# One branch on the count instead of four, over a loop through the four general passes

## What is computed

```python
h = h + moe(rmsnorm(h, g_ffn[l]), w_router[l], router_bias[l], w_gate[l], w_up[l],
            w_down[l], ws_gate[l], ws_up[l], ws_down[l])
return rmsnorm(h, g_final)
```

## Time and profile before

| | us |
|---|---|
| runs (3) | 1243.57, 1249.34, 1250.41 |
| median | 1249.34 |
| profiled execution, its own time | 1247.41 |
| its span, first to last instruction | 1245.6 |
| TensorE busy | 1100.4 (88%) |
| VectorE busy | 400.5 (32%) |
| ScalarE busy | 221.3 (18%) |
| GpSimd busy | 147.3 (12%) |
| mean granted clock of TensorE | 0.951 of full speed |

### The profile page before, as it was taken

How to read it: one execution, slowest core, us unless ns; L and a number is a source line. 1 busy time by engine, 2 the same in 40 slices (tenths; PEclk the granted TensorE clock), 3 DMA queues, 4 the chain that set the end, 5 groups by cost and what they waited for, 6 DMA issues and landing times.

```text
span 1245.6 us, 13250 instructions
## 1 busy us (share of the span) xinstructions
PE 1100.4 (88%) x5027; PEld 528.2 (42%) x5027; DVE 400.5 (32%) x927; ACT 221.3 (18%) x481; POOL 147.3 (12%) x194
## 2 busy tenths in 40 slices
PE   5999797887899969997999999997999889989745
PEld 3444585654444454443444343332433333423312
DVE  1883566353212031049522222221112122112127
ACT  3311432344102031031011111111111111101101
POOL 3000006020000000000212122121212111211100
PEclk9999798998899998999999999998999899989979
DMA  6234322320135400333399999999999999999387
GB/s 199 68 102 101 65 102 43 123 81 2 66 133 204 169 34 1 100 135 110 149 408 391 410 419 422 420 421 402 420 419 404 413 410 372 422 396 372 121 323 305
DMA packets 75821, 300.69 MB, mean 241 GB/s; under 512 B 20726, under 2 KB 24091, under 8 KB 50139
## 3 DMA queue, kind: packets, MB, share of 16 engines
q1 hardware_dynamic: 63066, 265.01, 54.7%
q0 software_dynamic: 12672, 34.62, 7.1%
HBM read 282.03 MB, written 27.53 MB: 249 GB/s over the span
## 4 chain that ended last, share of the span: by engine, by line
PE 76%; DMA 9%; DVE 6%; issue 4%; ACT 3%; SPq 1%; POOLq 0%; POOL 0%; DVEq 0%
PE ps L688 25%; PE ps L1070 22%; PE ps L1086 12%; PE ps L1052 3%; DMA ring<-in_w_down 3%; DMA dw<-in_w_down 3%; PE ps L812 2%; DMA ring<-expert_rows 2%; PE ps L825 2%; PE ps L671 1%; PE ps L1032 1%; PE ps L964 1%; PE ps L940 1%; PE ps L1094 1%; DMA z<-in_g_final 1%
## 5 line engine op out<-in xcount | busy, mean ns | idle before, releaser
L1070 PE MATMUL ps<-ring,z 128*32 128x512 f32 (+2 forms) x1056 | 270.9, 597 | 2.5 <-issue 1.3
L688 PE MATMUL ps<-dw,act_t 128*128 128x512 f32 x576 | 249.8, 595 | 3.1 <-issue 2.2
L688 PEld LDWEIGHTS ps<-dw,act_t 128*128 128x128 f32 x576 | 109.5, 191 | 140.0 <-issue 138.9
L1086 PE MATMUL ps<-ring,act_t 128*64 128x512 f32 (+2 forms) x528 | 146.8, 645 | 17.3 <-issue 14.5
L1070 PEld LDWEIGHTS ps<-ring,z 128*32 128x32 f32 (+2 forms) x1056 | 88.2, 134 | 115.4 <-issue 113.2
L1070 PE MATMUL ps<-z 128*32 128x512 f32 (+1 forms) x272 | 80.1, 603 | 4.9 <-issue 4.9
L1070 PE MATMUL ps<-dw,z 128*32 128x512 f32 (+2 forms) x272 | 77.7, 594 | 0.0
L1933 DVE COPY z<-ps 128x512 f32<-128x512 f32 x44 | 30.4, 692 | 139.7 <-PE ps L1086 139.7
L1086 PEld LDWEIGHTS ps<-ring,act_t 128*64 128x64 f32 (+2 forms) x528 | 44.3, 141 | 72.0 <-issue 68.3
L1411 ACT ACTIVATE tok<-ps 128x256 f32<-128x256 f32 x44 | 16.9, 384 | 307.4 <-PE ps L1070 307.4
L2065 POOL COPY ixb<-tabs 128x1 uint32<-128x1 uint32 x88 | 16.7, 190 | 411.1 <-DVE z L1933 393.3
(11 more groups left out here) (304 smaller groups left out, 1225.4 us busy)
## 6 DMA issues: line engine op xcount, KB each, us to landing
ring<-in_w_gate SPq DMA_DIRECT2D x44, 1024.0 KB
ring<-in_w_up SPq DMA_DIRECT2D x44, 1024.0 KB
ring<-in_w_down SPq DMA_DIRECT2D x44, 1024.0 KB, 29.1
ring<-expert_rows SPq DMA_DIRECT2D x8, 2048.0 KB, 21.7
dw<-in_w_gate SPq DMA_DIRECT2D x10, 1024.0 KB, 16.2
dw<-in_w_up SPq DMA_DIRECT2D x10, 1024.0 KB, 29.4
z<-in_w_gate SPq DMA_DIRECT2D x10, 1024.0 KB, 15.0
z<-in_w_up SPq DMA_DIRECT2D x10, 1024.0 KB, 28.5
```

The costliest lines, as they stand in the source:

```text
L688: ins = pe.matmul(ps[0:m, bank0 + j, 0:n], lhs(w, q * 4 + c4, c4, j), rhs(w, q * 4 + c4, c4, j), start=(q == 0 and c4 == 0), stop=(q == le ...
L1070: ins = pe.matmul(ps[rows, 2 + r % 2, :], xtt[r % 2][:, c, rows], ring_wgu(x % NBUF)[:, :, c, :], start=(c == 0), stop=(c == NC_D - 1))
L1086: ins = pe.matmul(ps[rows, 5 + n, :], htt[r % 2][:, c, rows], ring_wd(x % NBUF)[:, c, n * 512:(n + 1) * 512], start=(c == 0), stop=(c == 1))
```

## The change

The four branches of each engine, on the count over 0, 128, 256 and 384, become one branch on the count over 0. Under it stands a loop on the engine (`Fori`) through the four passes, so a pass number is a register's value, and what was worked out from it as a constant becomes sums of registers. If the count is above zero, all four passes run. Where a wait's target is now in a register, semaphore increments have been put behind some waits. On VectorE the table and address steps of a pass move into `pass_table`, which chains its steps by targets that depend on the pass; the calls outside the passes keep their steps, with `link` handed in. The core of the diff:

```diff
-    def slots_needed(eng):
-
-        return eng.value_load(ti[0:1, 0:1], min_val=0, max_val=S)
-
-    def needs_pass(eng, needed, p):
-
-        return eng.If(needed > SLOTS * p)
+    def needs_passes(eng):
+
+        return eng.If(eng.value_load(ti[0:1, 0:1], min_val=0, max_val=S) > 0)
...
         sp.wait_ge(s_cnti, 1)
-        needed = slots_needed(sp)
-        for p in range(PASSES):
-            with needs_pass(sp, needed, p):
-                if p == 0:
-                    sp.wait_ge(e_y, NR)
-                    sp.wait_ge(e_gu, NR)
-                    sp.dma_start(tv[0:NE, :], tvd).then_inc(s_tg, 16)
+        with needs_passes(sp):
+            sp.wait_ge(e_y, NR)
+            sp.wait_ge(e_gu, NR)
+            sp.dma_start(tv[0:NE, :], tvd).then_inc(s_tg, 16)
+            with sp.Fori(0, PASSES) as p:
                 with sp.Fori(0, NE // 4) as it:
                     for j in range(4):
-                        sp.wait_ge(e_y, it * 4 + (NR + NE * p - 3 + j))
+                        sp.wait_ge(e_y, p * NE + it * 4 + (NR - 3 + j))
                         load_expert(sp, it * 4 + j, j)
...
-        needed = slots_needed(pe)
-        for p in range(PASSES):
-            with needs_pass(pe, needed, p):
+        with needs_passes(pe):
+            with pe.Fori(0, PASSES) as p:
                 pe.wait_ge(s_srt, p + 2)
+                pe.sem_inc(s_pc, 1)
                 pe.transpose(ps[:, 0, 0:NE], ts_[0:NE, :], ident[0:NE, 0:NE]).then_inc(s_srf, 1)
                 pe.wait_ge(s_tab, p + 2)
                 one_pass(p)
...
-        needed = slots_needed(act)
-        for p in range(PASSES):
-            with needs_pass(act, needed, p):
+        with needs_passes(act):
+            with act.Fori(0, PASSES) as p:
                 one_pass(p)
...
-        def addresses(p):
-
-            dve.wait_ge(s_srf, p + 1)
-            if p == 0:
-                dve.tensor_copy(ecol, ps[:, 0, NE:NE + NR])
-                dve.tensor_copy(eid[:], ps[0:1, 0, 2 * NE:3 * NE])
-            else:
-                dve.wait_ge(s_idx, 2 * (NR + NE * (p - 1)))
-            n = NE if p else NR
+        def addresses(link, n):
+
...
             if n == 1:
-                addresses(0)
+                dve.wait_ge(s_srf, 1)
+                dve.tensor_copy(ecol, ps[:, 0, NE:NE + NR])
+                dve.tensor_copy(eid[:], ps[0:1, 0, 2 * NE:3 * NE])
+                addresses(link, NR)
...
+        LINKS = 2 * (2 * (SLOTS // 8) - 1 + 2)
+
+        def pass_table(p):
+
+            before, n = steps[0], [0]
+
+            def link_in_pass(ins):
+
+                n[0] += 2
+                ins.then_inc(s_dve, 1)
+                dve.wait_ge(s_dve, p * LINKS + (before + n[0] - 1))
+                dve.sem_inc(s_dve, 1)
+
+            slot_table(link_in_pass)
+            dve.wait_ge(s_srf, p + 2)
+            dve.wait_ge(s_idx, p * (2 * NE) + 2 * NR)
+            addresses(link_in_pass, NE)
+            assert n[0] == LINKS
...
-        needed = slots_needed(dve)
-        for p in range(PASSES):
-            with needs_pass(dve, needed, p):
-                if p == 0:
-                    dve.wait_ge(s_tg, 16 * (NT + 3))
-                slot_table()
-                addresses(p + 1)
+        with needs_passes(dve):
+            dve.wait_ge(s_tg, 16 * (NT + 3))
+            with dve.Fori(0, PASSES) as p:
+                pass_table(p)
                 one_pass(p)
...
         def one_pass(p):
-            base = NR + NE * p
+            base = p * NE + NR
             pool.wait_ge(e_xtr, base)
             pool.wait_ge(e_gc, base)
+            pool.sem_inc(s_gst, 1)
             for b in range(4):
-                gather(b, b, 2 * base + 1 + b)
+                gather(b, b, base * 2 + (1 + b))
...
         pool.wait_ge(s_cnti, 1)
-        needed = slots_needed(pool)
-        for p in range(PASSES):
-            with needs_pass(pool, needed, p):
-                if p == 0:
-                    all_scattered(NR)
+        with needs_passes(pool):
+            all_scattered(NR)
+            with pool.Fori(0, PASSES) as p:
                 pool.wait_ge(s_tab, p + 2)
+                pool.sem_inc(s_gst, 1)
                 one_pass(p)
         pool.sem_inc(s_rows, 1)
```

More of the change, by code:

```diff
@@ L1120, in one_pass @@
         def one_pass(p):
-            base, itb = NR + NE * p, NE // 4 * p
-            pe.wait_ge(xg_ld[0], 16 * (NR // 4 + NE // 4 * p + 1))
+            base, itb = p * NE + NR, p * (NE // 4)
+            pe.wait_ge(xg_ld[0], p * (4 * NE) + 16 * (NR // 4 + 1))
             for c in range(NC_D):
@@ L1129, in one_pass @@
                 for j in range(4):
-                    expert(it * 4 + (base + j), j, it + itb, again[j])
+                    expert(it * 4 + base + j, j, it + itb, again[j])
             for j in range(4):
-                expert(base + NE - 4 + j, j, itb + NE // 4 - 1, again[j], last=(j == 3))
-            down(3, [(ring_dn[3], 16 * (itb + NE // 4 + again[3])), (e_hte, base + NE), (e_yea, base + NE - 1),
-                     (e_yev, base + NE - 1)])
+                expert(base + (NE - 4 + j), j, itb + (NE // 4 - 1), again[j], last=(j == 3))
+            down(3, [(ring_dn[3], itb * 16 + 16 * (NE // 4 + again[3])), (e_hte, base + NE), (e_yea, base + (NE - 1)),
+                     (e_yev, base + (NE - 1))])
         pe.wait_ge(s_tab, 1)
@@ L1430, in one_pass @@
                 for j in range(4):
-                    expert(it * 4 + (base + j), j)
+                    expert(it * 4 + base + j, j)
             for j in range(4):
-                expert(base + NE - 4 + j, j, last=(j == 3))
-            down_out(base + NE - 1, 3)
+                expert(base + (NE - 4 + j), j, last=(j == 3))
+            down_out(base + (NE - 1), 3)
         act.wait_ge(s_tg, 16 * (NT + 2))
@@ L1891, in shared_hidden, with slot_table @@
                                      in1=sha[:, i, :], op0=ALU.mult, op1=ALU.mult).then_inc(s_shh, 1)
-        def slot_table(between=None):
+        def slot_table(link, between=None):
             for q in range(SLOTS // 8):
@@ L1916, in addresses @@
             dve.tensor_scalar(tabs[:, 0, 0:n], tabs[:, 1, 0:n], 3, None, ALU.logical_shift_right).then_inc(s_tab, 1)
-        slot_table(between=(4, 6, 8, 10))
+        slot_table(link, between=(4, 6, 8, 10))
         for n in range(2 * NT):
@@ L1983, in one_pass @@
                 for j in range(4):
-                    expert(it * 4 + (base + j), j, it * 4 + (D + j))
+                    expert(it * 4 + base + j, j, it * 4 + (D + j))
             for j in range(4):
-                expert(base + NE - 4 + j, j, D + NE - 4 + j, last=(j == 3))
-            down_out(base + NE - 1, 3)
+                expert(base + (NE - 4 + j), j, D + NE - 4 + j, last=(j == 3))
+            down_out(base + (NE - 1), 3)
         round_slots(0)
@@ L2114, in all_scattered @@
             for b in range(2):
-                pool.wait_ge(y_out[b], 8 * n)
+                pool.wait_ge(y_out[b], n * 8)
         def one_pass(p):
-            base = NR + NE * p
+            base = p * NE + NR
             pool.wait_ge(e_xtr, base)
             pool.wait_ge(e_gc, base)
+            pool.sem_inc(s_gst, 1)
             for b in range(4):
-                gather(b, b, 2 * base + 1 + b)
+                gather(b, b, base * 2 + (1 + b))
             for j in range(4):
@@ L2126, in one_pass @@
                 for j in range(4):
-                    expert(it * 4 + (base + j), j, it * 4 + j)
+                    expert(it * 4 + base + j, j, it * 4 + j)
             for j in range(4):
-                expert(base + NE - 4 + j, j, NE - 4 + j, tail=True)
+                expert(base + (NE - 4 + j), j, NE - 4 + j, tail=True)
             all_scattered(base + NE)
```

## The result

The changed kernel takes 1239.37 us (median of four runs, 1236.55 to 1240.23). The ratio to the kernel before is 0.9928 with a 95% interval of 0.9905 to 0.9952, so 9.0 us less, between 6.0 and 11.9. A second measurement, among the experiments, gave 0.9912 (0.9878 to 0.9945). The profiled execution spans 1237.3 us, its own time is 1239.09.

What follows compares the result with a forecast made beforehand. GpSimd's four branches were taken to hold the closing loads for 8.24 us, with the scatter's landing next. From 1248.4 us, a 4.85 us gain and nothing elsewhere gave 1243.5 us, 0.39% less; range 1238.5 to 1248.5.

Steps and rivals of the forecast that it cites:

- the sum's own bounds: Gain at the release: 3.2 us with the branch at 5.0 us, 5.05 with 0.42 and a 3.8 us landing.
- What bounds the kernel: Between last round and closing sum: an 11 us hole, where GpSimd's four branches hold the closing phase for 8.24 us.
- Step (a): GpSimd's branches before the closing loads: three of four go; the one left costs 2.58 us (0.42 to 5.0).
- step (b): SP's wait before the closing loads: the last scatter's 4.0 us landing becomes last in, so the gain is 4.85 us.
- Step (c): Branches of VectorE, ScalarE, TensorE and SP: covered or done early, so the same edit there is worth nothing.
- Step (e): First load of rows to the end: no step's work changes, so 56.7 us moves as a whole.
- The fourth rival: Start of the closing loads: less code being fetched there gives at most 1 us on top, 1242.4 us; chance 0.04.
- signs named for "right": Behind the last scatter: one branch per engine, landing ends SP's wait, load 4.1 us behind, 56.7 to end, TensorE 9 behind load.
- Step (d): New code inside the guard: not executed with a count not above zero, so it costs nothing.
- The first, an indirect DMA: GpSimd's queue behind the scatter: slow issue is the DMA's own work, only 0.8 us gained, 1247.6 us; chance 0.08.
- The second, a branch over 3.3 us: GpSimd's remaining branch replaces the landing as last; at 5.0 us the gain is 3.2, time 1245.2 us; chance 0.12.
- the third: GpSimd's remaining branch passes 8.24 us by loading code twice, 10.0 us: 1.8 us later, 1250.2 us; chance 0.03.

Runs made afterwards that it cites:

- all_far: Changed kernel with the four passes written out under the one branch instead of a loop, on every engine; ratio to the kernel before 0.9958 (0.9932 to 0.9984).
- pool_one: Kernel before with GpSimd's part alone taken from the changed kernel: one branch there, four on the other engines; ratio to the kernel before 0.9969 (0.9953 to 0.9984).
- pe_four: Changed kernel with TensorE's part alone put back to four branches; ratio to the kernel before 0.9971 (0.9952 to 0.9990).
- all_tiny: Changed kernel with three more branches on the count on every engine, each over a single semaphore increment; ratio to the kernel before 0.9941.
- gf_early: Changed kernel with SP issuing the load of g_final ahead of the waits for the scatters; ratio to the kernel before 0.9932 (0.9910 to 0.9955).
- sp_four: Changed kernel with SP's part alone put back to four branches; ratio to the kernel before 0.9867 (0.9829 to 0.9906).
- rows_first: Kernel before, all four branches kept, with GpSimd raising the closing loads' semaphore ahead of its branches; ratio to the kernel before 0.9972 (0.9950 to 0.9994).

## Why the prediction was right or wrong

The median of 1239.37 lies in the range of 1238.5 to 1248.5, near its low end, and 4 us under the 1243.5 forecast. That it lies inside is owed to the 4.8 us by which the range was widened for the scatter of runs: the gain of the edited part, 7.4 us, is outside the 3.2 to 5.05 that the sum's own bounds allow. "Within 0.5%" was held at 0.63 and "faster" at 0.34; measured is 0.72% faster, with an interval that reaches to 0.48%.

*What bounds the kernel.* Right: all that the profiles show of the gain lies behind the start of the last scatter, and in the kernel before GpSimd's branches held the release.

*Step (a), what GpSimd's remaining branch costs.* Taken at 2.58 us, measured about 0.5 (1179.6 to 1180.1). It was the low end, 0.42, that came true. Wrong in size and without effect, as step (b) had it: all_far, with 2.69, has the same release.

*Step (b), the landing is next.* Right in kind, and the row that was to show it is there (3.35 us behind the last scatter, then L642). The size was off: 4.0 us was read from a trace in which TensorE's code loads ran beside the scatter. With one branch on TensorE it is 3.35 us (3.61 in the second profile, 3.3 to 3.8 in all), with four there and one on GpSimd 4.01 (pool_one) and 5.20 (pe_four). Hence 5.55 us of release gained, not 4.85.

*Step (c), the other engines at nothing.* This is the step that failed. "They are covered, because TensorE waits for the first rows" leaves out what its branches do to the DMA engines: with TensorE alone at four the landing takes 1.85 us longer and the closing 2.4 us longer, 4.3 in all. It was short on TensorE's own time as well: had the branches stayed, the first sum was to be 0.6 us late, and in pool_one it is 3.69 us late. That the loads set the end all the same was right. ScalarE and VectorE cost another 1.9 us, all of it in the closing. Only SP's four are worth nothing (0.2 us, the scatter between two profiles).

*Step (e), the closing moves as a whole at 56.7 us.* Wrong by 1.8 us, for the reason of (c): 54.9. The fourth rival named this, code being fetched when the loads start, but held at 0.04 and capped at 1 us. It came nearest to what was found, at nearly twice its cap.

Of the signs named for "right", two came as told (one branch per engine, the wait ending with the landing), and three with other sizes: 3.43 us from last scatter to first load instead of 4.1, 54.9 to the end instead of 56.7, and TensorE's first sum 7.4 us behind the load instead of 9.

The parts don't add up to the whole: GpSimd 4.7, TensorE 4.3, ScalarE and VectorE 1.9 and SP 0.2, each against the changed kernel, are 11.1 us where all together are 7.4. They cover one another. While GpSimd's branches hold the loads back for 9 us, most of TensorE's code is loaded in a time when nothing else moves; with GpSimd's alone gone (pool_one) TensorE's loads meet the rows (five packets on q8 behind the first load instead of three) and 3.9 us is all that is won.

*Step (d), the guarded code costs nothing.* Nothing in the traces speaks against it.

*The rivals.* The first, an indirect DMA that slows GpSimd's queue, is dead: the changed kernel has the same DMA ahead of its branch and only 0.5 us behind it, and all_tiny has four branches there. The second, a branch over 3.3 us, did not happen, not even over four bodies, and so the third did not either.

*What stays open.* The edited part gives 7.4 us by the profiles; the two measurements say 9.0 and 11.0 us, with 7.4 inside the first interval (6.0 to 11.9) and inside the second (6.9 to 15.2). The second measurement was made to tell chance (0.994 expected) from a change in the stages ahead (0.9928 again); its 0.9912 (0.9878 to 0.9945) holds both. In the nine kernels with five runs or more, ratio and sum agree within 2.2 us to either side. Those with two to four runs all show more gain than their sum, which looks like chance but is not shown. The stages ahead, which do the same work in all these kernels (but for the early load of gf_early), end between 1171.5 and 1186.0 us in the fourteen profiles, so they scatter by more than what is missing. sp_four shows how much that can do: 0.9867 from two runs, with a sum that is the changed kernel's.

## What to carry to other kernels

A branch that is always taken is not free in the way of an instruction: the code at its target may have to be loaded, so branches in a row over long bodies should be merged, where one test can stand for all. (The signal can be put ahead of them only if what it announces does not depend on the bodies.) An engine off the critical path can still cost time through the code that it loads: look at the instruction queues' packets in the stretch, not only at who waits for whom. And a duration read beside other traffic (here the 4.0 us landing) is not the duration that is left when the change takes that traffic away.

## What the runs showed of the hardware

Branches over a single semaphore increment took 0.15 us on GpSimd and 0.21 to 0.24 us on TensorE. Over one pass body GpSimd's first took 0.4 to 0.5 us and its later ones 2.1 to 2.9 (3.4 once), and TensorE's 3.4 to 5.3. TensorE's fourth took 4.8 us where it began with the first load of rows (the two profiles of the kernel before), and 7.7 to 8.0 where it began 4.5 to 4.7 us behind it (pe_four, pool_one, rows_first). The time of such a branch on GpSimd did not grow from one body to four (2.69 us against 2.1 to 2.9). TensorE's code comes in packets of 16 KB, four of them for the last branches; beside them an indirect scatter landed after 4.0 to 5.2 us instead of 3.3 to 3.8, and SP needed 1.5 to 2.6 us for an issue that takes 0.4 to 0.8 otherwise. The Trainium skill ("Runtime: NRT & Kernel Launch", Instruction fetch mechanics) says that a taken branch whose target isn't loaded makes the engine wait for a load by DMA; all_tiny and all_far agree with that.
